# Layer norm of the convolution done one token tile at a time, with the output projection's first groups between the tiles

## The reference, cut to what matters

```python
glu = a_val * sigmoid(a_gate)
conv_out, new_buf = causal_depthwise_conv(buf, glu, conv_w, conv_b)   # width 31
ya = silu(layer_norm(conv_out, conv_ln_g, conv_ln_b))                 # per token, over 512 channels
...
yb = u * chunk_spatial_mix(v, w_s, b_s, chunk_len)
out = concatenate([ya, yb], axis=-1) @ w_out                          # 1024 x 1024
h = x + out
h = h + hierarchical_moe(rms_norm(h, norm_ffn_g), ...)
```

## Time and profile before

| | us |
|---|---|
| three runs | 700.38, 699.4, 700.95 |
| the profiled execution, its own time | 703.07 |
| the profiled execution, its span | 701.3 |

### The profile page before, as it was taken

How to read it: one execution, slowest core, us unless ns; L and a number is a source line. 1 busy time by engine, 2 the same in 40 slices (tenths; PEclk the granted TensorE clock), 3 DMA queues, 4 the chain that set the end, 5 groups by cost and what they waited for, 6 DMA issues and landing times.

```text
span 701.3 us, 10279 instructions
## 1 busy us (share of the span) xinstructions
PE 619.7 (88%) x3672; PEld 545.3 (78%) x3672; DVE 517.4 (74%) x568; ACT 356.5 (51%) x359; POOL 194.9 (28%) x190
## 2 busy tenths in 40 slices
PE   3899999963899978779999999999999999539994
PEld 3799999833799977568888888888888888339994
DVE  5558997997312258468999999999999999487445
ACT  6611322311521261457777777777777777424233
POOL 7035646930020000461222222222222211111004
PEclk9999999955799986889999999999999999859997
DMA  9973120234110141469999999999999999470003
GB/s 279 337 213 121 61 93 29 68 120 169 42 61 31 61 130 32 156 156 378 396 393 391 384 389 361 392 370 368 388 382 357 389 380 356 143 269 1 1 1 136
DMA packets 75659, 154.02 MB, mean 220 GB/s; under 512 B 8331, under 2 KB 25315, under 8 KB 75043
## 3 DMA queue, kind: packets, MB, share of 16 engines
q1 hardware_dynamic: 68075, 138.45, 55.4%
q0 software_dynamic: 5664, 10.08, 4.1%
q10 hardware_dynamic: 1888, 5.05, 2.1%
HBM read 147.90 MB, written 14.41 MB: 231 GB/s over the span
## 4 chain that ended last, share of the span: by engine, by line
PE 76%; DVE 10%; DMA 3%; POOL 3%; issue 3%; ACT 3%; SPq 1%; POOLq 0%; ACTq 0%; DVEq 0%
PE pair L1480 21%; PE pair L1482 20%; PE pair L1481 20%; PE pair L1532 8%; PE pair L1491 3%; DVE pair L1109 2%; DMA two<-in_state_conv 2%; POOL h L625 1%; PE pair L1747 1%; DVE lo L1065 1%; ACT act_hi L752 1%; POOL h L627 1%; PE pair L1654 1%; DMA raw<-pairs 1%; PE pair L1715 1%
## 5 line engine op out<-in xcount | busy, mean ns | idle before, releaser
L1480 PE MATMUL pair<-hi,act_hi 128*128 128x512 f32 (+2 forms) x828 | 291.7, 352 | 13.6 <-DVE lo L1065 4.0
L1482 PE MATMUL pair<-hi,act_lo 128*128 128x512 f32 (+2 forms) x828 | 284.9, 344 | 0.0
L1481 PE MATMUL pair<-lo,act_hi 128*128 128x512 f32 (+2 forms) x828 | 284.7, 344 | 0.0
L1065 DVE TENSOR_TENSOR lo<-raw,hi 128x2048 fp32r<-128x2048 f32 x110 | 249.0, 2290 | 35.4 <-ACT hi L752 35.2
L752 ACT ACTIVATE hi<-raw 128x2048 fp32r<-128x2048 f32 x119 | 225.0, 1917 | 82.3 <-PE pair L1482 44.8
L1480 PEld LDWEIGHTS pair<-hi,act_hi 128*128 128x128 f32 (+1 forms) x828 | 156.5, 189 | 36.6 <-issue 8.6
L1482 PEld LDWEIGHTS pair<-hi,act_lo 128*128 128x128 f32 (+1 forms) x828 | 155.9, 188 | 18.5
L1481 PEld LDWEIGHTS pair<-lo,act_hi 128*128 128x128 f32 (+1 forms) x828 | 156.7, 189 | 16.4
L1109 DVE SCALAR_TENSOR_TENSOR pair<-conv,vecs,pair 128x512 f32<-128x512 f32 x112 | 74.8, 747 | 0.0
L676 POOL DMA_INDIRECT pairs<-two,sidx x17 | 43.0, 2528 | 111.6 <-DVE two L1347 111.6
L752 ACT ACTIVATE act_hi<-pair 128x1024 fp32r<-128x1024 f32 (+3 forms) x49 | 38.4, 795 | 54.7 <-PE pair L1491 35.0
(11 more groups left out here) (194 smaller groups left out, 547.4 us busy)
## 6 DMA issues: line engine op xcount, KB each, us to landing
raw<-in_w_exp_gate SPq DMA_DIRECT2D x34, 1024.0 KB, 9.8
raw<-in_w_exp_up SPq DMA_DIRECT2D x34, 1024.0 KB, 9.0
raw<-in_w_exp_down SPq DMA_DIRECT2D x34, 1024.0 KB, 10.2
raw<-in_w_in SPq DMA_DIRECT2D x8, 1024.0 KB, 11.6
h<-in_x_prompt SPq DMA_DIRECT2D x8, 512.0 KB, 6.8
raw<-in_w_out SPq DMA_DIRECT2D x4, 1024.0 KB
raw<-in_w_ple_gate SPq DMA_DIRECT2D x4, 1024.0 KB, 9.8
raw<-pairs SPq DMA_DIRECT2D x4, 1024.0 KB, 8.0
```

The costliest lines, as they stand in the source:

```text
L1065: nc.vector.tensor_tensor(lo[:, n % SPLIT, :], raw[:, n % RAW, :], hi[:, n % SPLIT, :].bitcast(F32), ALU.subtract).then_inc(lo_dve, 1)
L1480: mm(out_, x_hi, w_hi, start=start, stop=False)
L1481: mm(out_, x_hi, w_lo, start=False, stop=False)
L1482: return mm(out_, x_lo, w_hi, start=False, stop=stop)
```

## The change

Step 2 and step 3 are done for one tile at a time, and step 4 for a tile no longer waits for the statistics of all. GpSimd gets `conv_deviation(t)`, which reads a tile's variance, clamps it and adds epsilon in one instruction, and raises it to -1/2: ten instructions on one column in place of two on five. VectorE's `variance(1)` goes; `bn_aggr` no longer waits for itself. VectorE's order over the tiles is written out by hand. On TensorE, tiles 0 to 2 are transposed back first; the transposes back of tiles 3 and 4 come behind output groups 0 and 1, and the eight state transposes behind group 2. The first addition to the residual, `out_add(0)`, with the wait for `x_again`, comes ahead of the low part of tile 4.

```diff
+            def conv_deviation(t):
+                r = rows(t)
+                g.wait_ge(var_done, t + 2)
+                nc.gpsimd.tensor_scalar(lr[0:r, 1, t:t + 1], mv[0:r, 1, t, 1:2], 0.0, EPS, ALU.max, ALU.add)\
+                    .then_inc(var_eps, 1)
+                g.wait_ge(var_eps, t + 2)
+                nc.gpsimd.tensor_tensor(lr[0:r, 1, t:t + 1], lr[0:r, 1, t:t + 1], half[0:r, :], ALU.pow)\
+                    .then_inc(sd_done, 1)
...
-            inverse_deviation(1)
+            for t in range(TILES):
+                conv_deviation(t)
             split_low(11)
...
-            for t in range(TILES):
+            def conv_stats(t):
                 r = rows(t)
                 v.wait_ge(ct_ps, t + 1)
                 link(nc.vector.bn_stats(st[0:r, 1, t, 0:6], bank[2 + t][0:r, :]))
-                link(nc.vector.bn_aggr(mv[0:r, 1, t, :], st[0:r, 1, t, 0:6]))
-            variance(1)
-            v.wait_ge(sd_done, 2)
-            for t in range(TILES):
-                r = rows(t)
+                nc.vector.bn_aggr(mv[0:r, 1, t, :], st[0:r, 1, t, 0:6]).then_inc(var_done, 1)
+
+            def conv_norm(t):
+                r = rows(t)
+                v.wait_ge(sd_done, t + 2)
                 if t >= 2:
                     v.wait_ge(cc_ps, t - 1)
...
+            conv_stats(0)
+            conv_stats(1)
+            conv_stats(2)
+            conv_norm(0)
+            conv_norm(1)
+            conv_stats(3)
+            conv_norm(2)
+            conv_stats(4)
+            conv_low(0)
+            conv_norm(3)
+            conv_low(1)
+            conv_norm(4)
+            conv_low(2)
+            conv_low(3)
+            v.wait_ge(x_again, 16 * TILES)
+            out_add(0)
+            conv_low(4)
...
             pe.wait_ge(yb_mul, TILES)
-            for t in range(TILES):
+            for t in range(3):
+                conv_back(t)
...
                 token_rows(t, n, bank[3 + q % 3], o_ps)
+                if i == 0 and t + 3 < TILES:
+                    conv_back(t + 3)
+                if (i, t) == (0, 2):
+                    state_rows()
```

More of the change, by code:

```diff
@@ L1207, in _, with conv_low @@
                     .then_inc(ct_norm, 1)
-            for t in range(TILES):
+            def conv_low(t):
                 r = rows(t)
@@ L1213, in _, with out_add @@
                                         ahi[:, 0:CB, t * P:t * P + r].bitcast(F32), ALU.subtract).then_inc(ya_lo, 1)
+            def out_add(q):
+                i, t = OUT_ORDER[q]
+                at = H[0:rows(t), t, i * UC:(i + 1) * UC]
+                v.wait_ge(o_ps, q + 1)
+                nc.vector.tensor_tensor(at, bank[3 + q % 3][0:rows(t), 0:UC], at, ALU.add).then_inc(o_add, 1)
+            conv_stats(0)
[15 more added lines that the diff above has]
+            conv_low(4)
             def ffn_norm(t):
@@ L1221, in ffn_norm @@
                 apply_norm(t, FFN, two[:, (t % 2) * D:(t % 2 + 1) * D]).then_inc(norm_done, 1)
-            v.wait_ge(x_again, 16 * TILES)
             for q, (i, t) in enumerate(OUT_ORDER):
-                at = H[0:rows(t), t, i * UC:(i + 1) * UC]
-                v.wait_ge(o_ps, q + 1)
-                nc.vector.tensor_tensor(at, bank[3 + q % 3][0:rows(t), 0:UC], at, ALU.add).then_inc(o_add, 1)
+                if q >= 1:
+                    out_add(q)
                 if i == 1 and t >= 1:
@@ L1620, in _, with conv_back @@
                 ins.then_inc(ct_ps, 1)
-            pe.wait_ge(yb_mul, TILES)
-            for t in range(TILES):
+            def conv_back(t):
                 r = rows(t)
@@ L1631, in _, with state_rows @@
                 ins.then_inc(cc_ps, 1)
[L1633 to L1639, removed]
+            def state_rows():
+                pe.wait_ge(fresh_done, 1)
+                for b in range(CB):
+                    ins = tr(bank[6][0:HIST, b * P:(b + 1) * P], G[:, b, GP - HIST:GP], ident[:, :])
+                ins.then_inc(state_ps, 1)
+                for b in range(CB):
+                    ins = tr(bank[0][0:SAMPLE, b * P:(b + 1) * P], fresh[:, b, :], ident[:, :])
+                ins.then_inc(state_ps, 1)
+            pe.wait_ge(yb_mul, TILES)
+            for t in range(3):
+                conv_back(t)
             def router_rows(t):
```

## The result

The change makes the kernel faster: 691.7 us median (690.71 to 693.84, 4 runs) against 700.08 (699.4 to 700.95, 4 runs), ratio 0.9875, 95% interval 0.9841 to 0.9909, so 1.2% with 0.9 to 1.6 as its bounds. The forecast was 694.4, range 691.8 to 697.4: the direction was right, the gain of 8.4 us is larger than the 6.0 of the sum, and the time lies 0.1 us under the range (two later medians of the changed kernel, 691.71 and 691.77, lie there too). TensorE's first group of the projection did not run at the half clock that the forecast charged it with.

The account below looks back on a forecast made before the run. Waits between engines bound from 164 to 182, then TensorE's own work. 173.5 + 14.25 + 2.23 + 1.74 + 0.1 = 191.8 against 197.86 is 6.0 us earlier; from median 700.38 that gives 694.4, range 691.8 to 697.4.

Parts of the forecast that it names:

- the sum: TensorE's work from group 0 on, added up: group 5 starts at 191.8 instead of 197.86, 6.0 us earlier.
- The start of group 0: First matmul of the projection on TensorE: at 173.5 instead of 182.38, 8.9 us earlier.
- The power step: GpSimd's power instruction on one column: priced 0.57 or 1.38 us in the trace; the lower was taken.
- TensorE from there: Groups 0 to 4: 14.25 us at full clock, plus 2.23 half clock, 1.74 for sixteen moved transposes, 0.1 changes of kind.
- the clock's term: Group 0's 24 matmuls on TensorE all at half clock: 2.23 us lost.
- Case (a): Rival: TensorE at full clock from early on, 0.5 to 2.2 of the 2.23 us not lost; 692.7 us, chance 0.25.
- unit 11's wait: TensorE's wait for unit 11 behind group 4: moves with the end of group 4, still about 1 us.
- (c): Rival: something behind group 4 is pinned elsewhere, so the 6 us are given back; 700.4 us, chance 0.04.
- (d): Rival: transposes between groups keep TensorE's clock at half to the end of block 0; 705.2 us, chance 0.06.

Follow-up runs that it names:

- late pair of runs: Changed kernel with eight extra power steps on GpSimd ahead of tile 0's deviation: TensorE idle meanwhile 696.51 us, filled with 44 unread transposes 695.49 us.
- tiles only: Kernel before with the change's tile-by-tile statistics, deviation and VectorE order, but all tiles and state rows transposed ahead of group 0: 693.54 us, again 694.44.
- three runs with fillings: Unread transposes in TensorE's idle: kernel before (698.82 us), changed kernel delayed on GpSimd (695.49), kernel before with only the change's TensorE order (696.26).
- before, idle filled: Kernel before plus 40 unread transposes in TensorE's idle and eight behind each transpose back but the last: 698.82 us, 0.9973 of before.

## Why the prediction came out as it did

**The start of group 0** was put at 173.5 - 165.67 = 7.8 us behind the first statistics, and is at 7.2. Two small terms were a little too dear: the pace of the statistics (0.85 a tile, not 0.95), and the transposes, which run at full clock: ScalarE starts 1.6 behind the first normalisation, not 2.08. The first silu, and the fourth, which waits behind group 0 as foreseen (0.34 of idle), in ScalarE's timeline:

```profile
170.04 1.51 ACT L881 ACTIVATE wide<-pair,vecs 128x128 f32<-128x128 f32 x4 [8.49 <-PE pair L1664]
...
176.67 1.51 ACT L881 ACTIVATE wide<-pair,vecs 128x128 f32<-128x128 f32 x4 [0.34 <-PE pair L1664]
```

**The power step** on one column was the cheap one of its two prices, all five times; timeline of GpSimd, tiles 0 and 4:

```profile
167.24 0.58 POOL L628 TENSOR_TENSOR lr<-lr,half 128x1 f32<-128x1 f32 x1
...
173.10 0.56 POOL L628 TENSOR_TENSOR lr<-lr,half 64x1 f32<-64x1 f32 x1
```

**TensorE from there** took 189.27 - 173.08 = 16.2 us to group 5. The sum without the clock's term is 14.25 + 1.74 + 0.1 = 16.1. So the transposes that were moved behind group 0 cost what was said, no group waited for VectorE or ScalarE, and the term that failed is one: "I take the whole of group 0 at half clock: 24 x (0.213 - 0.12) = 2.23 lost". It measured 0. With it and the start, 6.0 + 2.2 + 0.7 = 8.9 against 8.8 measured in the stage.

**Why that term was wrong.** The size was about right (1.9 us in the matmuls of the late pair of runs); the state of the clock was not. The argument for it was the stretch of 173 to 182 before, where TensorE works in pieces at half clock. But there the clock had fallen in the idle ahead (TensorE idle from 168.6, the clock down at about 171.4, a little later than the prediction read it) and the pieces did not raise it. After the change it is up when the pieces begin and still up at 173.08, when group 0 begins. Case (a) was this, with a chance of 0.25 and 692.7, of which it counted 1.7 of 2.23. The evidence for it was there and was ranked too low: the earlier trace rows showed the clock at 1.00 at 168, and the prediction's own schedule had the first transposes back at 169.3. The range was then cut 0.1 us too high: full clock and the earlier start together give 691.5.

It was not a safe case either. Pieces with short pauses did not hold the clock for good: in tiles only TensorE does the same first pieces, 3.5 us behind the first statistics as in the change, and goes on with tiles 3 and 4,

```profile
171.26 0.63 PE L1664 MATMUL pair<-ident,two 128*128 128x128 f32 x4 [1.43 <-DVE two L1216]
173.32 0.51 PE L1664 MATMUL pair<-ident,two 64*128 64x64 f32 x4 [1.43 <-DVE two L1216]
```

and the clock falls between 173 and 174, with no pause longer than 1.43 ahead of it. In the change group 0 begins before that point: 7.2 us behind the first statistics, where in tiles only 173 is 9.6 behind them. So in these traces the full clock in group 0 needed both parts, the early statistics and group 0 ahead of the rest.

The Trainium skill, "TensorE: Matmul & The Clock Gate", Part 4 (PE-mode transpose), says that transposes do not bring the full clock. Four traces had it at 1.00 behind or within a stretch with nothing but transposes on TensorE (before from 168, and the three runs with fillings), and in the stage the filled runs were faster by 1.9 to 2.8 us for it; the measurements decide.

**Behind the stage** the gain arrived whole: unit 11's wait is 1.03 us as before, ScalarE's first square comes 8.6 us earlier (199.87 for 208.46) behind the same 8.42 of idle, and `out_add(0)` did not wait for `x_again`. (c) and (d) did not happen; the transposes between the groups left the clock at 1.00.

## What to carry to other kernels

When a change closes an idle of TensorE, ask of each stretch behind it which clock it ran at and what the idle had done to that: closing the idle can pay twice, and the second payment (here 2.8 us of 8.8, by the kernel before with its idle filled) lies hidden in the busy time of before: only the granted clock shows it. Take the first piece of work that an engine's later bound needs, and move all that it doesn't need (state rows, later tiles) behind it. When several engines hand on to each other, reorder them together: TensorE's order alone, at full clock, gave 0.8. And look for the half of a sum that is ready early: here it was worth 5.6 us more.

## What the runs showed of the hardware

Transposes of f32 data alone raised the granted clock from 0.50 to 1.00 (before, at 168, where TensorE had run nothing else since 164.5), and back to back they held it there (1.00 from 168 to 173 in before, idle filled). Transposes in pieces did not do so for good: in tiles only the clock fell between 173 and 174, with pauses of at most 1.43 us between the pieces. At full clock four transposes took 0.44 us between groups (at 176.19), at half clock 0.96 and 0.85. The same kernel's clock can rise at another point of group 0: 2.6 and 4.2 us into it in two traces of before, worth 0.7 us. The kernel's front (to the first statistics) varied between 163.4 and 166.2 us and the router's stretch between 34.4 and 37.3, with no change in the code of either: the first pair of traces was 3.6 us further apart than the stage.
